# Second layer's mixer of a two-layer decoder: products of four blocks replaced by seven forms

## Chip, cores, metric

One NeuronCore of a Trainium2 chip runs the whole program. The metric is device time of one execution in microseconds (us), median of three runs. TensorE is PE in the rows, its weight loads PEld, VectorE DVE, ScalarE ACT, GpSimd POOL; SP issues the DMAs.

## The reference, cut to the part that changes

All is float32, 1024 tokens of width 1024. Layer 1 (the second) has a gated short convolution as its mixer:

```python
def short_conv_mixer(x, w_in, conv_w, w_out):          # layer 1
    proj = jnp.einsum('bsd,de->bse', x, w_in)          # 1024 x 1024 by 1024 x 3072
    gate_b, gate_c, h = jnp.split(proj, 3, axis=-1)
    z = gate_c * h
    zp = jnp.pad(z, ((0, 0), (CONV_WIDTH - 1, 0), (0, 0)))
    conv = sum(conv_w[k] * zp[:, k:k + s] for k in range(CONV_WIDTH))   # 3 taps
    return jnp.einsum('bse,ed->bsd', gate_b * conv, w_out)
...
for i in range(DEPTH):
    mix = ... if i % 2 == 0 else short_conv_mixer(...)
    x = layer_norm(DEEPNORM_ALPHA * x + mix, ln1_g[i], ln1_b[i])
    hid = jnp.square(jax.nn.relu(jnp.einsum('bsd,df->bsf', x, ffn_w1[i])))
    x = layer_norm(DEEPNORM_ALPHA * x + jnp.einsum('bsf,fd->bsd', hid, ffn_w2[i]), ln2_g[i], ln2_b[i])
    x = x + sigmoid(x @ ple_gate_w[i]) * (p[i] @ ple_w[i])
```

## The kernel before

**Products.** A float32 operand is split into a high part (ACT casts it to fp32r) and a low part (DVE or POOL subtracts the high part), and each 128x128 by 128x512 product is three matmuls: high by high, high by low, low by high (L1851 to L1853). Eight PSUM banks of 128x512 form two rings, `bank_a` and `bank_b`, of four.

**The two feed-forward layers** already use seven products in place of eight (a Strassen-Winograd scheme over 2x2 blocks). Their first product goes in *trips*: a trip makes 256 columns for all 1024 tokens by the seven products A11, S1, A22 (of the trip before), S2, A12, S4, S3, each 12 matmuls. The weight operand of each is one of the four quarters of the block (A..) or a sum of them (S..): S1 and S3 are summed on DVE, S2 and S4 on POOL; ACT makes the high part `op_hi`, POOL the low part `op_lo`. Five operand slots hold them, prepared four products ahead (`OP_LEAD`). The token operands are xt, its quarters, and four sums of them, `t_raw`/`t_hi`/`t_lo` 1 to 4. Three products accumulate on top of a bank that DVE must have read before, so PE waits: S4 for the read after S1, S3 for the read after S2, A22 for the second read of S3's bank. The results go to DRAM in seven forms (four quarters and three sums). Their second product is made of seven forms m1 to m7 whose operands are loaded back in *items* (`h_raw`, `w_raw`, split to `hop` and `wop`), five items in flight; m6, m5, m3 accumulate in the banks of the form before them, m4 in those of m7, so DVE must have added ("flushed") the form before to `resid` first.

**The mixer of layer 1** is done plainly before the change. For each of four blocks of 256 columns: gate_c (stage `c`, ACT copies it to `cv`), h (stage `h`, DVE multiplies and makes three taps of convolution), gate_b (stage `bgate`, DVE multiplies, splits into `hid_hi`, `hid_lo`), then the block's share of the output product goes to `bank_b` and DVE adds it to `resid` (stage `out`). Weight slabs are split by ACT (`w_hi`) and POOL (`w_lo`, L1007).

Each engine runs one list of stages in program order. An instruction that waits holds back all behind it on its engine. SP runs loads and spills in such a list as well.

```python
dve.tensor_tensor(z[:, k, o:o + HALF], bank_a[(st.ga + k) % RING][:, :], cv[:, k, s], ALU.mult)   # L1789
clink(dve.tensor_scalar(cv[:, k, s], z[:, k, o:o + HALF], tap[2], None, ALU.mult))                # L1792
clink(dve.scalar_tensor_tensor(out=cv[:, k, s], in0=z[:, k, o - 1:o - 1 + HALF], ...))            # L1793
clink(dve.scalar_tensor_tensor(out=cv[:, k, s], in0=z[:, k, o - 2:o - 2 + HALF], ...))            # L1795
```

## Time and profile before

| | |
|---|---|
| median of 3 runs | 2101.3 us (2101.21 to 2101.44) |
| span of the profiled execution | 2099.5 us, 25079 instructions |
| PE busy | 2088.8 us, 99%, 9605 instructions |
| DVE, ACT, POOL busy | 59%, 38%, 35% |
| mixer of layer 1 in the span | about 999 to 1354 us |
| mean granted TensorE clock | 1.000 |

For the profiled execution the profile gives its span alone; the median of the runs is 1.8 us above it. A matmul's busy time (389 ns) overlaps the next one's: what counts is the distance of their starts. The first column of a timeline row is its start in us, the second how long it took.

### The profile page before, as it was taken

How to read it: one execution, taken by the hardware profiler on the slowest of the kernel's cores; microseconds unless marked ns; L12 is line 12 of the kernel's file. 1: busy time of each engine (PE TensorE's matmuls, PEld its weight loads, DVE VectorE, ACT ScalarE, POOL GpSimd, SP SyncE). 2: the span in 40 equal slices, each digit the busy share in tenths (PEclk: the TensorE clock that was granted, in tenths of full speed). 3: DMA queues.
4: the chain of work that ended last, by engine and by line, in shares of the span. 5: the costliest groups of instructions: out<-in, count | busy, mean ns of one | idle time of the engine just before them, and what ended most of it. 6: DMA issues, size and time to landing. Idle time of an engine off the chain costs nothing.

```text
span 2099.5 us, 25079 instructions
## 1 busy us (share of the span) xinstructions
PE 2088.8 (99%) x9605; PEld 1735.1 (83%) x9605; DVE 1237.6 (59%) x1619; ACT 788.2 (38%) x1165; POOL 732.5 (35%) x493
## 2 busy tenths in 40 slices
PE   9999999999999999999999999999999999999999
PEld 9888788888888888888888888888888888888887
DVE  4744775565666657664543352675556566666563
ACT  3112454544543334531211101455444544334530
POOL 5113167778502000221422322268777512000220
PEclk9999999999999999999999999999999999999999
DMA  5111124344599555311121111124434599554221
GB/s 187 41 61 52 30 81 155 140 147 162 179 360 390 192 199 172 111 41 30 41 81 41 58 44 45 36 81 155 156 136 160 184 376 377 193 189 170 96 86 40
DMA packets 180819, 287.17 MB, mean 137 GB/s; under 512 B 12800, under 2 KB 71260, under 8 KB 180700
## 3 DMA queue, kind: packets, MB, share of 16 engines
q1 hardware_dynamic: 180000, 285.26, 39.6%
q8 instruction: 76, 1.25, 0.3%
q10 hardware_dynamic: 700, 0.31, 0.1%
q14 instruction: 43, 0.35, 0.1%
...
## 4 chain that ended last, share of the span: by engine, by line
PE 94%; POOL 2%; DVE 2%; issue 1%; ACT 1%; ACTq 0%; POOLq 0%; DVEq 0%
PE bank_a L1851 17%; PE bank_a L1853 17%; PE bank_a L1852 17%; PE bank_b L1851 14%; PE bank_b L1853 14%; PE bank_b L1852 14%; POOL op_lo L1021 1%; PE bank_a L1890 1%; PE bank_b L1890 1%; POOL op_sum L1094 1%; DVE xt_lo L1393 1%; DVE xt_hi L1388 0%; ACT op_hi L1249 0%; PE bank_a L2069 0%; PE bank_a L2078 0%
## 5 line engine op out<-in xcount | busy, mean ns | idle before, releaser
L1007 POOL TENSOR_TENSOR w_lo<-raw,w_hi 128x512 fp32r<-128x512 f32 x148 | 207.8, 1436 | 861.3 <-ACT w_hi L1115 861.2
L1851 PE MATMUL bank_a<-xt_hi,w_hi 128*128 128x512 f32 x640 | 251.4, 393 | 0.1
L1853 PE MATMUL bank_a<-xt_hi,w_lo 128*128 128x512 f32 x640 | 249.2, 389 | 0.0
L1852 PE MATMUL bank_a<-xt_lo,w_hi 128*128 128x512 f32 x640 | 249.1, 389 | 0.0
L1219 ACT CAST hop_hi<-h_raw 128x1024 fp32r<-128x1024 f32 x112 | 117.8, 1051 | 243.6 <-PE bank_a L1853 145.1
L1592 DVE TENSOR_TENSOR hop_lo<-h_raw,hop_hi 128x1024 fp32r<-128x1024 f32 x112 | 137.5, 1227 | 118.1 <-ACT hop_hi L1219 117.9
L1853 PE MATMUL bank_a<-wop_hi,hop_lo 128*128 128x512 f32 x512 | 199.2, 389 | 0.0
L1851 PE MATMUL bank_a<-wop_hi,hop_hi 128*128 128x512 f32 x512 | 199.2, 389 | 0.0
L1852 PE MATMUL bank_a<-wop_lo,hop_hi 128*128 128x512 f32 x512 | 199.2, 389 | 0.0
L1115 ACT CAST w_hi<-raw 128x512 fp32r<-128x512 f32 x148 | 82.4, 621 | 284.7 <-PE bank_a L1853 154.7
L1021 POOL TENSOR_TENSOR op_lo<-op_sum,op_hi 128x512 fp32r<-128x512 f32 x112 | 165.7, 1497 | 11.1 <-ACT op_hi L1249 6.7
L1249 ACT CAST op_hi<-op_sum 128x512 fp32r<-128x512 f32 x112 | 69.7, 622 | 227.1 <-POOL op_sum L1094 65.8
L1851 PE MATMUL bank_b<-wop_hi,hop_hi 128*128 128x512 f32 x384 | 150.0, 391 | 0.0
L1853 PE MATMUL bank_b<-wop_hi,hop_lo 128*128 128x512 f32 x384 | 149.5, 389 | 0.0
L1852 PE MATMUL bank_b<-wop_lo,hop_hi 128*128 128x512 f32 x384 | 149.4, 389 | 0.0
L1021 POOL TENSOR_TENSOR op_lo<-w_raw,op_hi 128x512 fp32r<-128x512 f32 x84 | 118.3, 1408 | 88.0 <-ACT op_hi L1249 87.0
L1851 PEld LDWEIGHTS bank_a<-xt_hi,w_hi 128*128 128x128 f32 x640 | 120.2, 188 | 26.1 <-DVE xt_lo L1393 0.9
L1853 PEld LDWEIGHTS bank_a<-xt_hi,w_lo 128*128 128x128 f32 x640 | 120.1, 188 | 25.2
L1852 PEld LDWEIGHTS bank_a<-xt_lo,w_hi 128*128 128x128 f32 x640 | 120.2, 188 | 24.7 <-issue 0.5
L1853 PE MATMUL bank_a<-xt_hi,op_lo 128*128 128x512 f32 x336 | 130.7, 389 | 0.0
L1851 PE MATMUL bank_a<-xt_hi,op_hi 128*128 128x512 f32 x336 | 130.7, 389 | 0.0
L1852 PE MATMUL bank_a<-xt_lo,op_hi 128*128 128x512 f32 x336 | 130.7, 389 | 0.0
...
## 6 DMA issues: line engine op xcount, KB each, us to landing
w_raw<-in_ffn_w_dram SPq DMA_DIRECT2D x144, 512.0 KB, 6.3
h_raw<-h_spill SPq DMA_DIRECT2D x112, 512.0 KB, 5.4
h_spill<-h_tile SPq DMA_DIRECT2D x170, 256.0 KB, 2.3
w_raw<-in_ffn_w_dram SPq DMA_DIRECT2D x112, 256.0 KB, 3.4
raw<-in_od_w_in_dram SPq DMA_DIRECT2D x48, 256.0 KB, 2.8
raw<-in_ple_gate_w_dram SPq DMA_DIRECT2D x32, 256.0 KB, 3.6
h_spill<-h_tile2t SPq DMA_DIRECT2D x28, 256.0 KB, 2.0
raw<-in_ev_w_in_dram SPq DMA_DIRECT2D x24, 256.0 KB, 3.2
```

Source lines behind the costliest of these rows:

```text
L1007: pool.tensor_tensor(lo, raw[:, n % NRAW, :], hi.bitcast(F32), ALU.subtract).then_inc(lo_split, 1)
L1021: pool.tensor_tensor(by_four(op_lo[s]), by_four(src) if src is not None else w1_quarter(b, op), by_four(op_hi[s]).bitcast(F32), ALU.subtra ...
L1094: pool.tensor_tensor(by_four(op_sum[s]), w1_quarter(b, "A12"), by_four(s2), ALU.subtract)\
L1115: act.copy(piece_place(slab, q)[0], raw[:, n % NRAW, :]).then_inc(hi_split, 1)
L1219: act.copy(hop_hi[k][:, :, :], h_raw[a.hop_chunk(i)][:, :, :]).then_inc(ahead_hi, 1)
L1249: act.copy(by_four(op_hi[s]), src).then_inc(op_high, 1)
L1393: dve.tensor_tensor(lo, staged(st, k), hi.bitcast(F32), ALU.subtract)\
L1592: dve.tensor_tensor(hop_lo[k][:, :, :], h_raw[a.hop_chunk(i)][:, :, :], hop_hi[k][:, :, :].bitcast(F32), ALU.subtract).then_inc(ahead_dve, 1)
L1851: pe.matmul(dst, s_hi, m_hi, start=first, stop=False, skip_group_check=on_top)
L1852: pe.matmul(dst, s_hi, m_lo, start=False, stop=False, skip_group_check=on_top)
L1853: return pe.matmul(dst, s_lo, m_hi, start=False, stop=last, skip_group_check=on_top)
L1890: ins = pe.transpose(dst[:, t * P:(t + 1) * P], src[:, st.half * HT + t, j * P:(j + 1) * P], ident[:, :])
```

## The change

The mixer of layer 1 takes the form of the feed-forward. The first 256 columns of gate_c and of h stay plain. The ten other blocks of the input product become trips, in the order b0, c1, h1, b1, c2, h2, b2, c3, h3, b3 (c: gate_c, h: h, b: gate_b, with the block's number). ACT and DVE evict each trip's quarters: c into `cv`, h into `z` (multiplied by `cv`, then 12 convolution instructions in the trip), b is multiplied by `cv`, and seven forms of it go to DRAM (`g_spill`). The output product is 14 items, two for each form. Trip b3 has S3 and S4 exchanged. The scaling of `resid` by alpha moves to POOL in trips 2 to 9, one tile in each.

```diff
+OD_TRIPS = (("b", 0),) + tuple((kind, blk) for blk in range(1, OD_BLOCKS) for kind in ("c", "h", "b"))
+OD_ITEMS = ([("m1", 0), ("m2", 0), ("m1", 1), ("m2", 1)]
+            + [(form, j) for form in ("m6", "m5", "m3", "m7", "m4") for j in range(OD_PAIRS)])
+OD_SLOTS = (0, 1, 2, 3, 4, 0, 1, 2, 3, 4, 0, 2, 1, 3)
...
+            per_trip = PER_TRIP if layer != OD or b < end - 1 else PER_TRIP[:5] + ("S3", "S4")
...
+    def short_conv():
+        turn = turns("gate", 1, list(range(KT)), ring="B", nested=True)
+        add("c", slab=("od", D), half=0, paced=True, split_next=True, inner=[turn])
+        add("tsum", layer=OD).unit = turn.unit
+        add("c", half=1, paced=True, last=True)
+        add("thi", layer=OD, half=1)
+        for i in (-4, -3, -2):
+            trip_step(OD, i)
+        add("thi", layer=OD, half=3)
+        add("h", slab=("od", 2 * D), half=1, load_next=False, split_next=False)
+        add("t4", layer=OD)
+        add("thi", layer=OD, half=2)
+        trip_step(OD, -1)
+        add("h", half=0, last=True)
+        for i, (b, op) in enumerate(tr.seq):
+            trip_step(OD, i)
+            if i == 1:
+                add("thi", layer=OD, half=4)
+            if op == "S2" and PLAIN < b <= PLAIN + TT:
+                add("alpha", tiles=[b - PLAIN - 1])
+            if b == last and op in ("S3", "S4"):
+                prepare(OD, ("S3", "S4").index(op))
+        nxt, form_heads = 2, {}
+        for i, (form, j) in enumerate(OD_ITEMS):
+            while nxt < len(OD_ITEMS) and (a.user_before(nxt) is None or a.user_before(nxt) < i):
+                prepare(OD, nxt)
+                nxt += 1
+            st = add("prod", item=i, layer=OD, head=form_heads.get(form))
...
-    for blk in range(OD_BLOCKS):
-        if blk == 0:
-            feature_halves("c", ("od", D), "gate")
-        else:
-            add("c", slab=("od", D + blk * BLK), half=0, blk=blk)
-            add("c", half=1, blk=blk, last=True)
-        add("h", slab=("od", 2 * D + blk * BLK), half=0, blk=blk)
-        add("h", half=1, blk=blk, last=True)
-        add("bgate", slab=("od", blk * BLK), half=0, blk=blk)
-        add("bgate", half=1, blk=blk, last=True)
-        block_out(("od_out", blk * BLK), ln=2 if blk == OD_BLOCKS - 1 else None)
+    short_conv()
...
+            def od_evictions(st):
+                if op == "S4":
+                    dve.wait_ge(trip_done, tr.done[b, op])
+                    od_wait(b, "u1")
+                    dve.tensor_tensor(q12, q12, bank, ALU.add).then_inc(od_step, 1)
+                    if kind == "h":
+                        od_wait(b, "c12")
+                        dve.tensor_tensor(q12, q12, cv_12[:, :], ALU.mult).then_inc(od_step, 1)
+                        od_wait(b, "m12")
+                        od_conv(b, blk, 0, 0)
+                        od_conv(b, blk, 0, 1)
```

Two places in DVE's program. First the h stage of the fourth block before and the same block's h trip after. Of before, `scratch` is both z and cv; two of four tiles are shown:

```order
L1789 TENSOR_TENSOR scratch<-bank_a,scratch 128x512
L1792 TENSOR_SCALAR scratch<-scratch,cols 128x512
L1793 SCALAR_TENSOR_TENSOR scratch<-scratch,cols 128x512
L1795 SCALAR_TENSOR_TENSOR scratch<-scratch,cols 128x512
L1789 TENSOR_TENSOR scratch<-bank_a,scratch 128x512
L1792 TENSOR_SCALAR scratch<-scratch,cols 128x512
L1793 SCALAR_TENSOR_TENSOR scratch<-scratch,cols 128x512
L1795 SCALAR_TENSOR_TENSOR scratch<-scratch,cols 128x512
```

After the change, from S4's eviction (`z<-z,bank_a`) to S3's (`z<-z,bank_b`) in an h trip:

```order
L1770 TENSOR_TENSOR z<-z,bank_a 128x512
L1773 TENSOR_TENSOR z<-z,cv_181 128x512
L1717 TENSOR_SCALAR cv_180<-z,cols 128x512
L1719 SCALAR_TENSOR_TENSOR cv_180<-z,cols,cv_180 128x512
L1722 SCALAR_TENSOR_TENSOR cv_180<-z,cols,cv_180 128x512
L1717 TENSOR_SCALAR cv_181<-z,cols 128x512
L1719 SCALAR_TENSOR_TENSOR cv_181<-z,cols,cv_181 128x512
L1722 SCALAR_TENSOR_TENSOR cv_181<-z,cols,cv_181 128x512
L1787 TENSOR_TENSOR z<-z,bank_b 128x512
L1791 TENSOR_TENSOR z<-z,cv_182 128x512
```

The read of S3's bank (`bank_b`) now stands behind one product with `cv` and six convolution instructions.

Second, the output product. Before, DVE comes from a gate_b stage straight to the 16 additions of a block:

```order
L1803 TENSOR_TENSOR tmp<-bank_a,scratch 128x512
L1388 CAST hid_hi<-tmp 128x512
L1393 TENSOR_TENSOR hid_lo<-tmp,hid_hi 128x512
L1636 TENSOR_TENSOR resid<-resid,bank_b 128x512 x16
L1789 TENSOR_TENSOR scratch<-bank_a,scratch 128x512
```

After, the rows ahead of the first flush, that of m1 (`t_od` is the weight sum of m6, `w_raw` with `t_od` that of m5, `hop_lo`, `wop_lo` the low parts of items 4, 5 and 6):

```order
L1978 TENSOR_TENSOR t_od_179<-w_raw_158,w_raw_164 128x1024
L1988 TENSOR_TENSOR hop_lo_138<-h_raw_153,hop_hi_133 128x1024
L1991 TENSOR_TENSOR wop_lo_148<-t_od_178,wop_hi_143 128x1024
L1980 TENSOR_TENSOR w_raw_159<-w_raw_159,t_od_178 128x1024
L1988 TENSOR_TENSOR hop_lo_134<-h_raw_154,hop_hi_129 128x1024
L1991 TENSOR_TENSOR wop_lo_144<-t_od_179,wop_hi_139 128x1024
L1980 TENSOR_TENSOR w_raw_160<-w_raw_160,t_od_179 128x1024
L1988 TENSOR_TENSOR hop_lo_135<-h_raw_155,hop_hi_130 128x1024
L1991 TENSOR_TENSOR wop_lo_145<-w_raw_159,wop_hi_140 128x1024
L2010 TENSOR_TENSOR resid<-resid,bank_a 128x512 x4
```

The flush now stands behind the preparation of items 2 to 6; the item that accumulates on its banks is item 4.

## Rows read from the trace of the kernel before

**Rows 1.** The page: span, and busy time of each engine.

```profile
span 2099.5 us, 25079 instructions
...
PE 2088.8 (99%) x9605; PEld 1735.1 (83%) x9605; DVE 1237.6 (59%) x1619; ACT 788.2 (38%) x1165; POOL 732.5 (35%) x493
```

**Rows 2.** Windows: mixer of layer 1, then trips of layer 0: busy per engine, clock.

```profile
1030.00:1340.00 310.00, 310.00 (x1370) 256.76 (x1369) 130.24 (x177) 42.43 (x76) 81.47 (x59) 1.00 0.18 54
360.00:555.00 195.00, 194.34 (x854) 159.23 (x853) 114.88 (x125) 96.56 (x165) 153.21 (x105) 1.00 0.45 156
```

**Rows 3.** PE's timeline in the mixer: first and last of 118 matmuls.

```profile
1014.66 0.39 PE L1851 MATMUL bank_a<-xt_hi,w_hi 128*128 128x512 f32 x1
...
1041.19 0.39 PE L1851 MATMUL bank_a<-xt_hi,w_hi 128*128 128x512 f32 x1
```

**Rows 4.** DVE's timeline: two tiles of the h stage, 1040 to 1053 us.

```profile
1042.17 0.49 DVE L1792 TENSOR_SCALAR scratch<-scratch,cols 128x512 f32<-128x512 f32 x1
1042.70 0.75 DVE L1793 SCALAR_TENSOR_TENSOR scratch<-scratch,cols 128x512 f32<-128x512 f32 x1
1043.49 0.75 DVE L1795 SCALAR_TENSOR_TENSOR scratch<-scratch,cols 128x512 f32<-128x512 f32 x1
...
1047.61 1.50 DVE L1792 TENSOR_SCALAR scratch<-scratch,cols 128x512 f32<-128x512 f32 x1
1049.14 1.66 DVE L1793 SCALAR_TENSOR_TENSOR scratch<-scratch,cols 128x512 f32<-128x512 f32 x1
1050.84 1.67 DVE L1795 SCALAR_TENSOR_TENSOR scratch<-scratch,cols 128x512 f32<-128x512 f32 x1
```

**Rows 5.** POOL's timeline over the same time: all of its work from 1028 to 1062.

```profile
1027.01 5.03 POOL L1007 TENSOR_TENSOR w_lo<-raw,w_hi 128x512 fp32r<-128x512 f32 x4
1047.53 6.13 POOL L1007 TENSOR_TENSOR w_lo<-raw,w_hi 128x512 fp32r<-128x512 f32 x4 [15.49 <-ACT w_hi L1115]
```

**Rows 6.** The chain that ended last, in one trip of layer 1's feed-forward.

```profile
1460.95 0.24 PE bank_a L1853
...
1461.25 0.60 ACT op_hi L1249
...
1461.92 1.35 POOL op_lo L1021
1463.27 1.71 POOL op_sum L1094
...
1465.04 1.64 POOL op_lo L1021
...
1466.82 0.47 PE bank_b L1851
```

**Rows 7.** DVE's timeline ahead of the trips of layer 1's feed-forward.

```profile
1392.62 5.49 DVE L1483 TENSOR_TENSOR t_raw<-xt_hi,t_raw 128x1024 f32<-128x1024 f32 x2 [8.57 <-PE bank_a L1853]
1398.15 5.55 DVE L1492 TENSOR_TENSOR t_lo<-t_raw,t_hi 128x1024 fp32r<-128x1024 f32 x2
1403.62 4.54 DVE L1498 TENSOR_TENSOR t_raw<-t_raw,xt_lo 128x1024 f32<-128x1024 f32 x2
...
1411.56 2.60 DVE L1492 TENSOR_TENSOR xt_lo<-t_raw,xt_hi 128x1024 fp32r<-128x1024 f32 x2 [1.10 <-ACT xt_hi L1129]
```

**Rows 8.** ACT's timeline there: the copies ahead of that last DVE row.

```profile
1410.47 2.00 ACT L1129 CAST xt_hi<-t_raw 128x1024 fp32r<-128x1024 f32 x2
```

**Rows 9.** DVE's timeline where layer 1's items are prepared.

```profile
1716.56 1.22 DVE L1595 TENSOR_TENSOR wop_lo<-w_raw,wop_hi 128x1024 fp32r<-128x1024 f32 x1
1717.70 1.22 DVE L1592 TENSOR_TENSOR hop_lo<-h_raw,hop_hi 128x1024 fp32r<-128x1024 f32 x1
```

**Rows 10.** DMA issues: KB each and median us to landing.

```profile
h_raw<-h_spill SPq DMA_DIRECT2D x112, 512.0 KB, 5.4
h_spill<-h_tile SPq DMA_DIRECT2D x170, 256.0 KB, 2.3
```

**Rows 11.** One load of six within five us, and the cast that waited for it.

```profile
1686.69 1.00 SPq L833 DMA_DIRECT2D h_raw<-h_spill  x1
...
1694.66 1.05 ACT L1219 CAST hop_hi<-h_raw 128x1024 fp32r<-128x1024 f32 x1 [0.35 <-DMA h_raw<-h_spill]
```

**Rows 12.** Windows at the end of the span, where PE has stopped: clock.

```profile
2097.00:2099.00 2.00, 0.00 (x0) 0.00 (x0) 0.05 (x1) 0.00 (x0) 0.00 (x0) 0.79 0.35 131
```

More of the change, by code:

```diff
@@ L213, in spilled, with pair, slot, hop_chunk @@
         return 16 * (self.layer * (FFN_BLOCKS - PLAIN) + blk - PLAIN + 1)
+class OdAhead(Ahead):
+    def pair(self, i):
+        return self.items[i][1]
+    def slot(self, i):
+        return OD_SLOTS[i]
+    def hop_chunk(self, i):
+        return OD_HOP_AT[i]
+    def w_chunk(self, load):
+        return OD_W_AT[load]
 class Trips:
@@ L242, in __init__ @@
             if op in ("S2", "S4"):
-                self.sum_pool[b, op] = layer * 2 * blocks + len(self.sum_pool) + 1
+                self.sum_pool[b, op] = base["sums"] + len(self.sum_pool) + 1
+            if op == "A11":
+                self.move[b] = base["moves"] + len(self.move) + 1
+            if layer == OD:
+                kind = OD_TRIPS[b - PLAIN][0]
+                for name in (OD_STEPS[kind] if b < end - 1 else OD_LAST).get(op, ()):
+                    self.step[b, name] = len(self.step) + 1
+                if op == "A12" and kind == "c":
+                    self.copied[b] = len(self.copied) + 1
+                continue
@@ new lines, in first_read, with make_trips, make_ahead @@
+    def first_read(self, b, op):
+        name = {"S4": "s15", "S3": "u1", "A22": "c22"}[op]
+        return ("odstep", self.step[b, name]) if self.layer == OD else ("hid", self.hid[b, name])
+def make_trips():
+    trips, before = {}, None
+    for layer, end in ((0, FFN_BLOCKS), (OD, PLAIN + len(OD_TRIPS)), (1, FFN_BLOCKS)):
+        trips[layer] = before = Trips(layer, before, end)
+    return trips
+def make_ahead():
+    first = FfnAhead(0, None, ITEMS, PAIRS, True)
+    mixer = OdAhead(OD, first, OD_ITEMS, OD_PAIRS, False)
+    return {0: first, OD: mixer, 1: FfnAhead(1, mixer, ITEMS, PAIRS, True)}
@@ L260, in make_plan @@
     held = {"A": [None] * RING, "B": [None] * RING}
-    trips = [Trips(layer) for layer in range(2)]
-    ahead = [Ahead(layer) for layer in range(2)]
+    trips, ahead = make_trips(), make_ahead()
     need = dict(xu=[0, 0], hu=[0, 0])
@@ L285, in add @@
         if kind == "prod" and args["head"] is None:
-            adds["ga" if FORMS[ITEMS[args["item"]][0]][0] == "A" else "gb"] = adds["flu"] = HT
+            adds["ga" if FORMS[ahead[args["layer"]].items[args["item"]][0]][0] == "A" else "gb"] = adds["flu"] = HT
         if args.get("ring") == "B":
@@ L452, in prepare @@
     def prepare(layer, n):
-        if n + 1 < len(ITEMS):
+        if n + 1 < len(ahead[layer].items):
             add("wsum", item=n + 1, layer=layer)
@@ L531, in trunk @@
     plan, trips, slab_end, slabs, total, ends = make_plan()
-    ahead = [Ahead(layer) for layer in range(2)]
-    heads = [{ITEMS[st.item][0]: st for st in plan if st.kind == "prod" and st.layer == layer and st.head is None}
-             for layer in range(2)]
+    ahead = make_ahead()
+    heads = {layer: {a.items[st.item][0]: st for st in plan
+                     if st.kind == "prod" and st.layer == layer and st.head is None} for layer, a in ahead.items()}
     n_slabs = total["slab"]
@@ L875, in stage @@
             def stage(st):
-                if st.kind == "slab":
+                if st.kind == "slab" and st.layer == OD:
+                    sp.wait_ge(ahead_dve, ahead[OD].sum[5])
+                elif st.kind == "slab":
                     sp.wait_ge(ahead_dve, ahead[st.layer].dve[LAST_FORM - 1])
@@ L1042, in stage @@
                     split_low(st.cur + 2, st.piece + 6, 4, at=1)
-                if st.kind == "wsum" and ITEMS[st.item][0] == "m6":
+                if st.kind == "wsum" and ahead[st.layer].items[st.item][0] == "m6":
                     a, i = ahead[st.layer], st.item
@@ L1596, in stage @@
                                       ALU.subtract).then_inc(ahead_dve, 1)
-                if st.kind == "prod" and ITEMS[st.item][1] == PAIRS - 1:
-                    form, head = ITEMS[st.item][0], st.head
+                if st.kind == "prod" and ahead[st.layer].items[st.item][1] == ahead[st.layer].pairs - 1:
+                    form, head = ahead[st.layer].items[st.item][0], st.head
                     if form == "m1":
```

583 lines of the change are left out of this document (425 added, 158 removed).

## The prediction

> **What bounds the kernel now.** I read the page first: PE is busy 2088.8 of 2099.5 us, and no other engine over 59% [rows 1]. The windows say the same of this mixer: 310 of 310 us busy, clock 1.00, with DVE at 42% and POOL at 26% [rows 2]. Then PE's timeline, for what a matmul costs. Its row says 389 ns, but the starts are closer: 118 matmuls in a row start between 1014.66 and 1041.19 us, 26.53 / 117 = 0.2267 us apart [rows 3]. That distance is the price of a matmul here, since PE issues one after another with no gap. In the whole mixer I found no pause of PE over 0.2 us. So a matmul removed from the mixer shortens the span in full, unless PE then waits, and every wait of PE is new time.
>
> **What is removed.** A plain block of the input product is 96 matmuls, a trip 7 x 12 = 84; ten blocks save 120. The output product goes from 384 to 14 x 24 = 336 and saves 48. The order confirms 168 fewer. 168 x 0.2267 = **38.1 us**. The plain mixer's casts and slab splits go too, but they lie beside PE and give nothing.
>
> **What is added** lies on DVE, POOL, ACT and SP. A product takes 12 x 0.2267 = 2.72 us and a trip 19.05 us, an item 5.44 us. I go through the four places where PE can come to wait.
>
> *DVE beside POOL.* The convolution shows its price twice: 0.49, 0.75 and 0.75 us with POOL idle, 1.50, 1.66 and 1.67 us at 1047 to 1052 [rows 4], when POOL works without a break [rows 5]. In the mixer before, that is rare. In trips POOL is busy 153.2 of 195 us, 79% [rows 2], so this is what the h trips run in. With starts 0.04 apart, a tile's three instructions are 2.1 us alone and 4.9 us beside POOL; two tiles at a share of 79% go at a speed of 0.21 + 0.79 x 2.1 / 4.9 = 0.55, so 4.2 / 0.55 = 7.6 us.
>
> The Trainium skill (SBUF — State Buffer, "Who interferes with whom") says that a VectorE instruction with two SBUF inputs and a GpSimd instruction that reads SBUF exclude each other for the whole instruction, the second one waiting until the first ends. The rows agree that both lose, but four of POOL's went from 5.03 to 6.13 us, and one of DVE's from 0.75 to 1.67. By the rule each of DVE's would wait out one of POOL's and take 1.26 + 0.75 = 2.0 us, two tiles some 9 us instead of 7.6, which over three h blocks is an estimated 4 us more.
>
> *1. The first trip: 8 us.* Ahead of the feed-forward's trips DVE needs 1392.62 to 1408.1 = 15.5 us for six large instructions, from the end of the third plain half block on [rows 7]. The new mixer has the same six at the same place (end of the first half of h), plus one z product ahead and two behind (0.6 each, a read of PSUM), then 12 convolution instructions, 8.4 us at the price alone, since POOL runs out of work then. Only behind them stand the sum for S3 and the eviction of S1: 15.5 + 1.8 + 8.4 + 1.2 = 26.9 us. PE has 10.9 us of the plain half block, then A11, S1, S2, A12, and wants S4 at 21.8. Wait 5.1. Behind it ACT makes S3's high part and two large copies of 2.0 us [rows 8], DVE the two `xt_lo` that follow (2.6) [rows 7] and the eviction of S2: S3 waits 2 to 3 more, and the next S1 some 0.5. Bounds: 5, if DVE's six go at their price alone (about 7 us); 11, if the convolution runs beside POOL.
>
> *2. The h trips: 7 us.* After S4 ends DVE does its eviction 0.6, the product 1.2, two tiles 7.6, then reads S3's bank 0.6: 10.0 us. A22 needs that read, and PE has three products, 8.16 us, until then: 1.9 us of wait, and some 0.4 on the operand of the next S1, whose sum is queued on DVE as well. The second half (behind A22: 0.6, 1.2, 7.6, 0.6 against 8.16 us until S3) has the slack that the first wait made. I take 2.3 for each of three blocks. Bounds: nothing at the price alone (0.6 + 0.7 + 4.2 + 0.6 = 6.1 < 8.16), and with POOL busy all the time 0.6 + 1.6 + 9.8 + 0.6 = 12.6, 4.4 us twice in a block, 26 us. In c and b trips DVE has 6 to 17 us of work in 19, so delays don't add up.
>
> *3. The last trip: 2.5 us.* In the feed-forward the path to S2's operand takes 1460.95+0.24 to 1466.82 = 5.6 us for two products of PE, 5.44: it is just at its limit [rows 6]. It goes through POOL's sum and two low parts. With S3 ahead of S4 the sum for S4 has its slot one product later, and S3's own low part, from DVE's sum, comes ahead on POOL: 1.2 + 0.6 + 1.35 + 1.71 + 1.64 and gaps of 0.3 are 6.8 after A11, with DVE late from h3: 1.4 to 3.5 us of wait.
>
> *4. The output product: 12 us.* Item 4 (m6) accumulates on m1's banks, and could start 4 x 5.44 = 21.8 us after the last A22. DVE must flush m1 first, in the order given, after preparing items 2 to 6. Item 3 needs the form that the last A22 makes: DVE reaches it about 5.6 us after A22 ends (three sums and item 1's preparation are ahead), the spill takes 2.3, its load 5.4 by the median [rows 10], but 1694.66 - 1686.69 = 8 when six are under way [rows 11], and here it is followed by six or more; with the cast that is 17.5 us. Then DVE works through item 3, the weight sums of 5, 6 and 7 and items 4, 5, 6: 11 instructions at 1.14 apart [rows 9], 12.5 us, so the first flush ends at 30.7: item 4 is 9 us late, of which 3.4 already at item 3. Weights of items 5 and 6, last in the same burst, may cost 1 or 2 more. Then DVE is behind, and m5, which needs m6's flush, waits about 2. Sum 12. Bounds: 4, if loads land at the median and nothing is ahead on DVE; 18, if the burst adds another 6. Afterwards DVE has some 9.5 us of work in 10.9 us of PE for each form and keeps up. The layer norm behind it follows the last additions by the same instructions as before, and costs nothing new.
>
> *5. The clock: 2 us.* Before, PE never paused; only when it had ended did the granted clock fall, to a mean of 0.79 in the window 2097 to 2099 [rows 12]. A pause of 6 to 9 us ahead of item 4 may let it fall too, to 1.2 GHz. From no fall (0) to a stretch at half speed as long as the pause (4.5): I take 2. The page TensorE: Matmul & The Clock Gate (The Trainium skill, "What's actually happening") gives 1.2 and 2.4 GHz as the two levels and idleness as what leads to the lower; no row here shows how it comes back.
>
> Sum: -38.1 + 8 + 7 + 2.5 + 12 + 2 = -6.6. The profiled span 2099.5 would become 2092.9, and the median, 1.8 above, **2094.7, say 2095 us**.
>
> **Rivals.** *The waits are mostly hidden* (0.15). POOL pauses whenever PE does, so DVE's work runs near the price alone, and loads land in time: 5 + 0 + 1.4 + 6 + 0 = 12.4, 26 us faster, about 2078; with half of that, 2085. Against it stands that in the trips POOL is busy 79% and that the order behind A22 is fixed.
>
> *The convolution beside POOL takes over* (0.20). Place: the h trips. If DVE is served at 4.9 us a tile throughout, the waits there are up to 26 in place of 7, the sum is +12 and the time 2114. It decides from where an h block costs over (38.1 + 4.2 - 24.5) / 3 = 5.9 us. For it: every DVE row beside a busy POOL is at the high price. Against it: POOL has only five slots of lead and must stop when PE stops.
>
> *Each pause costs the clock* (0.10, within the case above and the next). Seven pauses of 2 to 8 us; if PE then runs at half speed for as long as each, the 29.5 us of waits bring 15 more in place of 2, and the time is 2108.
>
> *Gain and waits cancel* (0.20): waits of 34 to 42 us, 2097 to 2105, by the upper half of the bounds of places 1 and 4.
>
> **How the numbers follow.** Within 0.2% (4.2 us) I could not tell a change. The forecast, 2085 to 2097, has 0.45, the hidden case 0.15: faster 0.6. Cancelling 0.2. Slower 0.2, from convolution and clock. The range leaves out about 0.1 on either side: 2081 to 2108; the likeliest case alone is 2085 to 2097.
>
> **What would show it.** PE 168 instructions fewer; PE idle of some 30 us in place of 2, with its releasers DVE evictions (S4, S3 of b0; A22 of h1 to h3), POOL's `op_lo` (S2 of b3), and ahead of items 3, 4 and m5 DVE's `wop_lo` and flush. The convolution's rows between 1.0 and 1.67 us in trips. The granted clock below 1.00 in a window behind item 4. Wrong it would be by convolution rows at 0.5 to 0.8 us, by an item 4 that starts with no wait, or by waits of PE for loads or spills in the trips, of which I see none.

## The result and the profile after

The changed kernel takes **2114.6 us** (median of 4 runs, 2113.2 to 2116.8), the kernel before 2101.3 on the same chip: a ratio of 1.0065, 95% interval 1.0051 to 1.0079. It is slower by 13.3 us, where 2095 was forecast. The page, beside [rows 1]:

```profile
span 2111.6 us, 25132 instructions
...
PE 2067.5 (98%) x9437; PEld 1712.4 (81%) x9437; DVE 1328.9 (63%) x1689; ACT 835.3 (40%) x1215; POOL 810.8 (38%) x533
```

PE has 9437 instructions, 168 fewer, and the gain of 38.1 us is real: its busy time fell by 21.3 us although much of what is left ran slower. It was paid back inside the mixer. Before, PE had no pause there. Now its timeline has eleven. Each row is the first matmul behind one; the bracket is the wait and what ended it (two of the eleven, 3.14 and 1.02 us, repeat those at 1124 and 1143 and are left out):

```profile
1031.89 0.80 PE L2232 MATMUL bank_a<-xt_hi,w_hi 128*128 128x512 f32 x1 [6.42 <-POOL w_lo L1246]
1068.06 0.50 PE L2232 MATMUL bank_a<-xt_hi,op_hi 128*128 128x512 f32 x1 [1.84 <-DVE b L1752]
1079.99 0.47 PE L2232 MATMUL bank_a<-t_hi,op_hi 128*128 128x512 f32 x1 [1.83 <-POOL op_lo L1260]
1124.20 0.79 PE L2232 MATMUL bank_b<-xt_hi,op_hi 128*128 128x512 f32 x1 [3.13 <-DVE z L1787]
1143.28 0.47 PE L2232 MATMUL bank_a<-t_hi,op_hi 128*128 128x512 f32 x1 [1.06 <-POOL op_lo L1260]
...
1248.15 0.50 PE L2232 MATMUL bank_b<-xt_hi,op_hi 128*128 128x512 f32 x1 [0.32 <-DVE z L1787]
1254.55 0.77 PE L2232 MATMUL bank_b<-t_hi,op_hi 128*128 128x512 f32 x1 [3.38 <-POOL op_lo L1260]
1290.61 0.56 PE L2232 MATMUL bank_b<-wop_hi,hop_hi 128*128 128x512 f32 x1 [3.20 <-DVE wop_lo L1991]
1305.97 0.77 PE L2232 MATMUL bank_a<-wop_hi,hop_hi 128*128 128x512 f32 x1 [8.03 <-DVE resid L2010]
```

The waits are 33.4 us. By the distances of starts, with 0.2267 taken off each, they are 35.1. The rest is behind them. PE's timeline after the wait of 3.13 us:

```profile
1124.80 0.63 PE L2233 MATMUL bank_b<-xt_lo,op_hi 128*128 128x512 f32 x1
1125.22 0.63 PE L2234 MATMUL bank_b<-xt_hi,op_lo 128*128 128x512 f32 x1
...
1127.46 0.40 PE L2234 MATMUL bank_b<-xt_hi,op_lo 128*128 128x512 f32 x1
1127.70 0.39 PE L2232 MATMUL bank_b<-xt_hi,op_hi 128*128 128x512 f32 x1
```

Matmuls start 0.43 us apart, not 0.23, from 1124.2 to 1127.2: half speed, 1.4 us lost. The same in the windows (columns: from and to, length, busy of PE, PEld, DVE, ACT, POOL with counts, granted clock, DMA share, GB/s):

```profile
1032.00:1040.00 8.00, 8.00 (x30) 6.52 (x31) 1.40 (x3) 1.25 (x2) 5.97 (x4) 0.82 0.43 133
1040.00:1055.00 15.00, 15.00 (x68) 12.43 (x67) 10.47 (x7) 1.14 (x2) 9.30 (x5) 1.00 0.00 0
...
1254.00:1262.00 8.00, 7.46 (x21) 5.92 (x22) 6.58 (x7) 1.84 (x2) 3.51 (x3) 0.61 0.10 23
...
1306.00:1312.00 6.00, 6.00 (x16) 4.73 (x17) 6.00 (x12) 0.00 (x0) 0.00 (x0) 0.55 1.04 393
1312.00:1320.00 8.00, 8.00 (x37) 6.62 (x36) 8.00 (x11) 2.31 (x3) 0.00 (x0) 1.00 0.93 325
```

From 1306 to 1312 PE is busy all the time and does 16 matmuls in 6 us, behind it 37 in 8. Seven pauses (the six of over 3 us and that of 1.84 us at 1068) have such a *slow stretch*: they lose 1.5, 1.7, 1.4, 1.6, 2.7, 1.7 and 2.6 us, 13.3 together. With some single slow starts, the loss against the kernel before is some 14 us in all (matmuls that start over 0.2267 us apart without a pause, summed over the span: some 24 us against 10). So -38.1 + 35.1 + 14 = +11, of 12.1 us by which the span of the profiled execution grew; 1 us of it isn't placed.

| place | us predicted | us in the trace |
|---|---|---|
| `h`'s slab, ahead of the trips | none | 6.4 |
| first trip | 8 | 3.7 |
| h trips | 7 | 8.7 |
| last trip | 2.5 | 3.4 |
| output product | 12 | 11.2 |
| clock | 2 | 13.3 to 14 |

**The pause nobody looked for.** PE waits 6.4 us for the low part of `h`'s slab. POOL's timeline there, four instructions of 128x512, and DVE's at the same time, eight sums of 128x1024:

```profile
1015.88 15.96 POOL L1246 TENSOR_TENSOR w_lo<-raw,w_hi 128x512 fp32r<-128x512 f32 x4 [64.52 <-ACT w_hi L1354]
```

```profile
1017.88 2.35 DVE L1850 TENSOR_TENSOR t_raw<-t_raw,xt_hi 128x1024 f32<-128x1024 f32 x2
...
1024.69 2.35 DVE L1864 TENSOR_TENSOR t_raw<-tmp,t_raw 128x1024 f32<-128x1024 f32 x2
```

POOL's four took 5.0 to 6.1 us before [rows 5] and take 16.0 here. The mean of 4.0 hides how: windows of POOL alone (busy time with count, granted clock, DMA) over this row:

```profile
1015.90:1028.10 12.20, 12.20 (x1) 1.00 0.00 0
1028.20:1031.80 3.60, 3.60 (x3) 0.50 0.00 0
```

The first of the four takes 12.3 us, from 1015.9 to 1028.2, and ends 1.1 us after the last of DVE's sums (1027.0); the other three take 1.26 each. So one instruction was held for as long as DVE had such work without a gap. DVE loses nothing: 1.14 us for each sum. In [rows 4] it was DVE that lost most.

**In an h trip** DVE's timeline from S4's eviction to the read of S3's bank, the order shown ahead of the prediction:

```profile
1112.95 0.69 DVE L1770 TENSOR_TENSOR z<-z,bank_a 128x512 f32<-128x512 f32 x1 [2.03 <-PE bank_a L2234]
...
1114.87 1.40 DVE L1717 TENSOR_SCALAR cv<-z,cols 128x512 f32<-128x512 f32 x1
1116.31 0.75 DVE L1719 SCALAR_TENSOR_TENSOR cv<-z,cols,cv 128x512 f32<-128x512 f32 x1
1117.09 1.66 DVE L1722 SCALAR_TENSOR_TENSOR cv<-z,cols,cv 128x512 f32<-128x512 f32 x1
...
1123.47 0.67 DVE L1787 TENSOR_TENSOR z<-z,bank_b 128x512 f32<-128x512 f32 x1
```

Six convolution instructions take 8.6 us here (7.6 were forecast), the next six 4.7.

**In the output product**, ahead of item 4, DVE:

```profile
1289.32 1.23 DVE L1991 TENSOR_TENSOR wop_lo<-w_raw,wop_hi 128x1024 fp32r<-128x1024 f32 x1
1294.92 1.23 DVE L1978 TENSOR_TENSOR t_od<-w_raw,w_raw 128x1024 f32<-128x1024 f32 x1 [4.37 <-POOL w_raw L1287]
...
1304.01 1.21 DVE L1991 TENSOR_TENSOR wop_lo<-w_raw,wop_hi 128x1024 fp32r<-128x1024 f32 x1
1305.15 2.47 DVE L2010 TENSOR_TENSOR resid<-resid,bank_a 128x512 f32<-128x512 f32 x4
```

DVE stands still for 4.4 us for a weight that landed late (POOL's sum of it starts only at 1292.4), does nine instructions for items 4 to 7, and only then flushes m1, which PE had finished at 1287.

### The profile page after: what moved, and what is told of

Its sections match the earlier page's. It is cut to its first block and busy times, and to the rows that moved or that the text cites. A ratio compares the mean times of both kernels' runs of the same rounds, so it can differ in the third digit from the quotient of the medians.

```text
span 2111.6 us, 25132 instructions
## 1 busy us (share of the span) xinstructions
PE 2067.5 (98%) x9437; PEld 1712.4 (81%) x9437; DVE 1328.9 (63%) x1689; ACT 835.3 (40%) x1215; POOL 810.8 (38%) x533
## 5 line engine op out<-in xcount | busy, mean ns | idle before, releaser
L1246 POOL TENSOR_TENSOR w_lo<-raw,w_hi 128x512 fp32r<-128x512 f32 x92 | 140.7, 1561 | 736.3 <-ACT w_hi L1354 736.3
L1260 POOL TENSOR_TENSOR op_lo<-op_sum,op_hi 128x512 fp32r<-128x512 f32 x152 | 222.5, 1480 | 42.6 <-ACT op_hi L1525 36.6
L2232 PE MATMUL bank_a<-xt_hi,op_hi 128*128 128x512 f32 x456 | 178.3, 391 | 1.8 <-DVE b L1752 1.8
L2233 PE MATMUL bank_a<-xt_lo,op_hi 128*128 128x512 f32 x456 | 178.1, 391 | 0.0
L2232 PE MATMUL bank_a<-xt_hi,w_hi 128*128 128x512 f32 x320 | 127.6, 399 | 6.4 <-POOL w_lo L1246 6.4
L2232 PEld LDWEIGHTS bank_a<-wop_hi,hop_hi 128*128 128x128 f32 x576 | 108.8, 189 | 30.8 <-DVE wop_lo L1991 8.4
L1991 DVE TENSOR_TENSOR wop_lo<-w_raw,wop_hi 128x1024 fp32r<-128x1024 f32 x108 | 132.6, 1228 | 0.6
L2233 PEld LDWEIGHTS bank_a<-wop_lo,hop_hi 128*128 128x128 f32 x576 | 108.8, 189 | 22.7
L2234 PEld LDWEIGHTS bank_a<-wop_hi,hop_lo 128*128 128x128 f32 x576 | 108.7, 189 | 22.8
L2232 PE MATMUL bank_b<-t_hi,op_hi 128*128 128x512 f32 x304 | 120.4, 396 | 5.0 <-POOL op_lo L1260 4.9
```

Source lines behind the costliest of these rows:

```text
L1246: pool.tensor_tensor(lo, raw[:, n % NRAW, :], hi.bitcast(F32), ALU.subtract).then_inc(lo_split, 1)
L1260: pool.tensor_tensor(by_four(op_lo[s]), by_four(src) if src is not None else w1_quarter(b, op), by_four(op_hi[s]).bitcast(F32), ALU.subtra ...
L1991: dve.tensor_tensor(wop_lo[k][:, :, :], w2_source(a, i), wop_hi[k][:, :, :].bitcast(F32), ALU.subtract).then_inc(ahead_dve, 1)
L2232: pe.matmul(dst, s_hi, m_hi, start=first, stop=False, skip_group_check=on_top)
L2233: pe.matmul(dst, s_hi, m_lo, start=False, stop=False, skip_group_check=on_top)
L2234: return pe.matmul(dst, s_lo, m_hi, start=False, stop=last, skip_group_check=on_top)
```

## Experiments

The theory: each wait is a place in the order of DVE's or POOL's queue, and each pause of some length has a slow stretch of its own. The rivals: DVE's (or the loads') sum of work is the limit, so that a wait removed comes back elsewhere; and the clock's loss is something else than the pause.

### Four edits of order, one at a time

**Flush m1 ahead of items 4 to 6.**

```diff
-            while nxt < len(OD_ITEMS) and (a.user_before(nxt) is None or a.user_before(nxt) < i):
+            while nxt < len(OD_ITEMS) and (a.user_before(nxt) is None or a.user_before(nxt) < i) \
+                    and not (nxt >= 4 and i < 3):
```

> DVE flushes m1 right behind the preparation of item 3; items 4, 5 and 6 are prepared behind it. Theory (item 4 waits for the flush's place in DVE's order): item 3 ends as before; DVE is done with item 3 at 1290.6 us, flushes m1 until 1293.0, must then still wait for the weight sum of item 5 (POOL, at 1294.9), and has item 4 ready at 1298.4, so PE's wait ahead of item 4 falls from 8.0 to about 2.3 us, and with it the slow stretch behind it (2.6 us over full speed) to 1 or less: 2107 us. Rival A (the clock costs nothing of its own, only waits count): 2109 us. Rival B (the late loads hold item 4, not the order): the wait stays at 8 and the time at 2114.6.

Measured: 2113.7 us (2110.2 to 2114.2), ratio to before 1.0054 (1.0037 to 1.0071). PE's waits at items 4 and 6:

```profile
1299.61 0.50 PE L2233 MATMUL bank_a<-wop_hi,hop_hi 128*128 128x512 f32 x1 [0.56 <-DVE wop_lo L1992]
...
1317.50 0.77 PE L2233 MATMUL bank_a<-wop_hi,hop_hi 128*128 128x512 f32 x1 [6.71 <-DVE resid L2011]
```

The place was right, 8.0 became 0.6. But the flush of m6 stands behind items 7 and 8 and m2's flush in the same queue, and PE, now earlier, meets it.

**In the h trips, read S3's bank ahead of the convolution**, and the last quarter of it behind S2's read of the b trip.

```diff
...
                         dve.tensor_tensor(q12, q12, cv_12[:, :], ALU.mult).then_inc(od_step, 1)
-                        od_wait(b, "m12")
-                        od_conv(b, blk, 0, 0)
-                        od_conv(b, blk, 0, 1)
...
                         dve.tensor_tensor(q22, q22, cv_22[:, :], ALU.mult).then_inc(od_step, 1)
+                        od_wait(b, "m12")
+                        od_conv(b, blk, 0, 0)
+                        od_conv(b, blk, 0, 1)
...
```

> In the h trips the convolution of the first half stands behind the read of S3's bank, and the last quarter of the convolution behind the first read of the next trip's S2. Same instructions, other order. Theory (the order of the reads costs the 3.1 + 3.1 + 0.3 us ahead of A22 and the 1.1 + 1.0 ahead of the next S1, and each 3.1 us wait a slow stretch of 1.4 to 1.6 us behind it): all of it goes, 8.6 + 3.0 us: 2103 us. Rival (DVE as a whole is the limit in an h trip, so the wait only moves to the next read or operand sum): 2112 to 2115 us, with PE released by DVE at other lines.

Measured: 2116.8 us (2115.7 to 2118.5), 1.0075 (1.0060 to 1.0090). The waits of 3.13 us ahead of A22 are gone, and waits of 0.8 and 3.4 us stand in their place, the second for POOL's low part of the next S1: its sum, on DVE, was behind nine convolution instructions. As the rival said of the place, though the convolution in quarters, further down, shows that it was order all the same. Behind the wait of 3.40 us at 1144.9 no slow stretch follows, behind the next, 3.37 us at 1206.9, one of 1.7 us does.

**Undo the exchange in the last trip** (S4 ahead of S3 again).

```diff
-            per_trip = PER_TRIP if layer != OD or b < end - 1 else PER_TRIP[:5] + ("S3", "S4")
+            per_trip = PER_TRIP
...
```

> The last trip has S4 ahead of S3 again, like all others; preparation of items 0 and 1, spills and loads keep their places in time. Theory (the exchange puts S2's operand on a path of 6.8 us against 5.44): the 3.4 us wait ahead of S2 of b3 and the slow stretch of 2.7 us behind it go: 2108.5 us. Rival (that wait is DVE's and POOL's delay out of h3, not the exchange): wait of 2 to 3.4 us stays, 2113 to 2115 us. Another: the spills and items behind come later by as much as was won, and item 3 waits 6 us in place of 3: no change.

Measured: 2114.3 us (2114.1 to 2115.9), 1.0064 (1.0049 to 1.0079), no change. The 3.38 us ahead of S2 of b3 are gone, but these stand in PE's timeline, at A22 of h3 (0.32 before) and A22 of b3 (none before):

```profile
1251.04 0.80 PE L2229 MATMUL bank_b<-xt_hi,op_hi 128*128 128x512 f32 x1 [3.13 <-DVE z L1785]
1269.37 0.50 PE L2229 MATMUL bank_b<-xt_hi,op_hi 128*128 128x512 f32 x1 [1.73 <-DVE b L1785]
```

**DVE's eight sums behind POOL's split.**

```diff
                     if st.layer == OD:
                         dve.wait_ge(unit_lo, st.need_x[0])
+                        dve.wait_ge(lo_split, st.piece + 4)
```

> DVE starts the eight sums for t_raw only when POOL has split the h slab. Theory (POOL's four splits take 16 us because DVE's 128x1024 sums stand beside them; alone they take about 1.25 each): POOL is done at 1021, PE has no wait ahead of the first h matmul (6.4 us less) and no slow stretch behind it (1.5 less), and DVE, idle from 1027 to 1037.8 before, loses nothing: 2106.7 us. Rival (that wait paid in advance for the first trip, whose waits of 2.1, 1.8 and 1.8 us now grow by as much, since DVE's work there sets the end): 2113 to 2116 us.

Measured: 2110.2 us (2108.2 to 2111.8), 1.0042 (1.0027 to 1.0057). POOL's row, and PE's waits in the first trip:

```profile
1014.99 6.95 POOL L1246 TENSOR_TENSOR w_lo<-raw,w_hi 128x512 fp32r<-128x512 f32 x4 [64.53 <-ACT w_hi L1354]
```

```profile
1054.83 0.47 PE L2233 MATMUL bank_b<-t_hi,op_hi 128*128 128x512 f32 x1 [3.06 <-POOL op_lo L1260]
1064.60 0.50 PE L2233 MATMUL bank_a<-xt_hi,op_hi 128*128 128x512 f32 x1 [2.42 <-DVE b L1752]
1076.58 0.47 PE L2233 MATMUL bank_a<-t_hi,op_hi 128*128 128x512 f32 x1 [1.70 <-POOL op_lo L1260]
```

The four splits take 7.0 in place of 16.0 us by this edit alone, and the pause of 6.4 us is gone: DVE's sums had starved POOL. (The first still takes 3.2 us: DVE's subtractions ahead of the sums go on until 1017.1, and it ends 1.1 us behind them.) The first trip's waits rose from 3.7 to 7.2 us, so about half was an advance payment. Between the two theories: 4.4 us won, of 7.9.

### Further along the same queues

**Convolution of block 0 behind S2's read of the first trip**, on top of the last one.

```diff
+            if i == 2:
+                add("conv0")
...
```

> The edit of the run with the sums behind the split, and besides it the twelve convolution instructions of block 0 stand behind the read of S2's bank of the first trip, not ahead of S3's operand sum and of the read of S1's bank. Theory (those twelve, 11 us from 1052 to 1063, are what S4 and the next S1 wait for, 2.4 and 1.7 us): both waits and the slow stretches behind them go, about 6 us against that run's 2110.2: 2104 us; a wait of 3 us ahead of the first S2 stays, since it is for POOL's low part. Rival (DVE's sum of work up to the second trip is the limit, whatever its order): the waits come back at S3, A22 or the next S1, and the time is 2109 to 2111 us.

Measured: 2111.9 us (2110.8 to 2116.3), 1.0057 (1.0042 to 1.0072). The theory fell, and the rival named the place rightly: the read of S1's bank makes nobody wait any more, but twelve instructions in one piece now stand ahead of the next S1's sum, and PE waits 5.2 us there in place of 1.7. That DVE's sum of work is the limit doesn't follow: with the same instructions in quarters ("More of the same order", below) the two waits of this part are 4.1 and 1.1 us.

**Spread the convolution of the h trips**, a quarter at a time, over the h and the b trip.

```diff
+def conv_tiles(b, op, kind, end):
+    if kind == "h":
+        return ("10", "11") if op == "A22" and b == end - 2 else ()
...
+    return {"S1": ("01",), "A12": ("10",) if b < end - 1 else (), "S4": ("11",) if b < end - 1 else ()}.get(op, ())
```

> The convolution of an h trip is spread: one quarter behind S3's eviction, one behind S1's of the b trip, one behind A12's and one behind S4's there (in h3 the last two stay where they are). Same instructions. In the run with the convolution later, the operand sum for the next S1 came at 1137.6 instead of 1128, behind nine convolution instructions, and PE waited 3.4 us for the low part made from it. Theory (order, not amount: in an h and a b trip together DVE has work for about 31 of 38 us): no operand sum or bank read stands behind more than three convolution instructions, so the waits of the h trips (3.1, 1.1, 3.1, 1.0, 0.3) go with their slow stretches (3.0): 2103 us, or 2106 if the wait ahead of S2 of b3 grows. Rival (DVE beside POOL is too slow for any order): 2113 to 2117 us.

Measured: 2106.5 us (2104.8 to 2108.7), 1.0026 (1.0016 to 1.0036). The waits of the first two h blocks, 8.4 us, are down to 1.67 twice, behind which no slow stretch follows. The window of h1 and b1, of the changed kernel, then of this one:

```profile
1106.00:1163.00 57.00, 52.81 (x226) 42.88 (x225) 40.58 (x42) 12.68 (x22) 37.92 (x27) 0.97 0.27 87
```

```profile
1106.00:1163.00 57.00, 55.33 (x244) 45.52 (x243) 39.91 (x43) 14.57 (x25) 41.70 (x30) 1.00 0.27 88
```

18 matmuls more in the same 57 us, with DVE busy for 40 of them in both: order, not amount.

**Both flushes**, m1's and m6's, ahead of what isn't needed yet (`and not (nxt >= 8 and i < 6)` besides).

> As in the run with the flush first, and besides it items 8 and later are prepared only behind the flush of m6. In that run the wait of 8.0 us ahead of item 4 fell to 0.6, but 6.7 us came up ahead of item 6, which accumulates on m6's banks, flushed only behind items 7 and 8 and m2. Theory (order in DVE's queue): the flush of m6 now comes at 1311, and item 6 waits about 1 us; sum of both waits 1.6 in place of 8.0, with 2 us of slow stretch less: 2106 us. Rival (DVE has 25 us of work without a break from 1296 on, so what is pushed back is late at the next place): a wait of 4 to 6 us ahead of item 7, 8 or 9, 2112 us.

Measured: 2113.7 us (2108.1 to 2113.9), 1.0053 (1.0036 to 1.0070). The waits at items 4 and 6 are 0 and 0.9 us, as expected, and one of 3.5 us comes up at m4, whose banks hold m7: DVE had the layer norm's statistics of the first tiles ahead of m7's flush and waited for ACT's squares. The output product waits 7.9 us in place of 11.2. That isn't to be seen in the time: in the same trace the slow stretches of the trips are longer (2.8 and 3.0 us behind the pauses of 3.13 us, where the changed kernel's trace has 1.4 and 1.6). The edit doesn't touch the trips; what makes them longer isn't shown.

**All four together.**

> The four edits of order together: sums behind the split, convolution of block 0 behind S2's read, convolution of the h trips spread, both flushes ahead of later items. Nothing is computed otherwise. If the waits are separate costs, the gains add: 4.4 + 6 + 9 to 12 + 8.5 = 28 to 31 us, 2084 to 2087 us, faster than the kernel before by 0.7%, and the gain from 168 matmuls fewer is there to see. Rival (DVE's backlog is handed from place to place, so that each wait removed shows up behind): 2095 to 2105 us.

Measured: 2100.9 us (2098.8 to 2102.5), 0.9999 (0.9990 to 1.0008). 14 us less than the change, half of the forecast. 26.7 us of waits are left by the starts' distance, among them those that the single edits had created.

### The clock, measured by itself

**Eight long pauses in the kernel before.** POOL makes 2 to 14 small instructions on unused memory when a stage ends, and PE waits for them:

```diff
+                if (st.kind, st.half, st.blk) in PAUSES:
+                    pool.wait_ge(a_full, st.ga)
+                    for n in range(PAUSES[st.kind, st.half, st.blk]):
+                        pool.wait_ge(paused, before_pause(st) + n)
+                        pool.tensor_scalar(sig[:, 0, :], sig[:, 0, :], 1.0, 1.0, ALU.mult, ALU.mult)\
+                            .then_inc(paused, 1)
...
+                if (st.kind, st.half, st.blk) in PAUSES:
+                    pe.wait_ge(paused, before_pause(st) + PAUSES[st.kind, st.half, st.blk])
```

> The kernel before, with eight pauses of PE put into its mixer, two per block (ahead of h and of gate_b), the rest as it was: PE waits until POOL has made 2, 3, 4, 5, 6, 8, 10 and 14 instructions of some 0.55 us on unused memory behind the end of the stage before, 52 in all, some 30 us of pause. Theory (a pause of about 3 us or more costs a stretch at half clock of 3 to 6.5 us, whatever its length, 1.5 to 2.9 us): six or seven of the eight have one, about 14 us in all: 2101 + 30 + 14 = 2145 us. Rival A (the prediction's: a stretch as long as the pause, or none for short ones, with the mean 2 us in 30): 2133 us. Rival B (half clock for as long as each pause, so the loss grows with it): 2101 + 30 + 15, with 0.5 us behind the shortest and 4 behind the longest.

Measured: 2207.8 us (2205.8 to 2209.2), 1.0506 (1.0491 to 1.0522). POOL splits a slab ahead of its small instructions, which the expectation forgot, so the pauses are 8.4 to 16.5 us, 88.4 in sum. The shortest and the longest in PE's timeline, and windows behind them:

```profile
1032.67 0.79 PE L1866 MATMUL bank_a<-xt_hi,w_hi 128*128 128x512 f32 x1 [8.35 <-POOL sig L1047]
...
1413.61 0.80 PE L1866 MATMUL bank_a<-xt_hi,w_hi 128*128 128x512 f32 x1 [16.50 <-POOL sig L1047]
```

```profile
1032.50:1038.50 6.00, 5.83 (x14) 4.57 (x15) 0.00 (x0) 0.00 (x0) 0.11 (x1) 0.50 0.13 39
1413.50:1417.50 4.00, 3.89 (x9) 3.12 (x10) 0.00 (x0) 0.00 (x0) 0.06 (x1) 0.50 0.00 0
1418.00:1425.00 7.00, 7.00 (x33) 5.76 (x32) 1.81 (x3) 0.00 (x0) 0.00 (x0) 1.00 0.01 2
```

Behind all eight PE runs at 0.50 of 2.4 GHz, 1.2 GHz, for 3.1 to 6.1 us, then at 1.00. In order of the pauses (8.4, 8.8, 8.9, 10.2, 10.3, 12.3, 13.1, 16.5) the losses are 3.0, 1.6, 2.8, 2.4, 2.6, 2.9, 1.5, 2.0 us, some 18.7 together. They don't grow with the pause: rival B falls, and so does A. The forecast times all fell short, since the pauses came to 88 us and not 30; 2101 + 88 + 19 = 2208 us is what was measured.

**Sixteen pauses, meant short.** The same edit, three instructions at each of sixteen places.

> The kernel before with the same sum of pause in sixteen short ones: three POOL instructions, about 1.9 us, ahead of each half of h and of gate_b in all four blocks. Theory (a pause of up to 2 us has no slow stretch behind it): 16 x 1.9 = 30 us and no loss of clock: 2131 us, granted clock 1.00. Rival (the loss goes with the time paused): as much as with the long ones, 2145 us.

Measured: 2219.3 us (2216.9 to 2220.9), 1.0561 (1.0545 to 1.0577). For the same reason only the eight at second halves are short, 2.2 and 2.7 us by turns, so the test of 1.9 us isn't made. Behind the eight of 8.2 to 9.1 us there is always a slow stretch, behind those of 2.7 us three times in four, of 2.2 us once in four. Windows behind pauses of 2.21, 2.21 and 2.73 us:

```profile
1049.00:1052.50 3.50, 3.37 (x8) 2.70 (x9) 1.36 (x2) 0.00 (x0) 0.07 (x1) 0.52 0.00 0
1168.90:1172.40 3.50, 3.50 (x15) 2.91 (x16) 1.23 (x2) 0.00 (x0) 0.00 (x0) 1.00 0.00 0
...
1319.00:1322.50 3.50, 3.32 (x8) 2.67 (x9) 0.00 (x0) 0.00 (x0) 0.13 (x1) 0.54 0.00 0
```

**The long pauses filled** with unused products (beside the kernel with empty pauses; `FILL` is 34 to 70 products):

```diff
+                    pe.wait_ge(b_free, st.bread)
+                    for _ in range(FILL[st.kind, st.half, st.blk]):
+                        pe.matmul(bank_b[RING - 1][:, :], xt_hi[0][:, 0, 0:P], xt_hi[0][:, 0, :], start=True, stop=True)
                     pe.wait_ge(paused, before_pause(st) + PAUSES[st.kind, st.half, st.blk])
```

> The kernel before with the eight long pauses (8.4 to 16.5 us, 90 us in all, 2207.8 us, eight slow stretches of 1.5 to 3.0 us behind them, 17 us together), and in each pause PE makes 34 to 70 unused products of 128x128 by 128x512 on a free PSUM bank before it waits, so that it stands still for about 0.5 us only. Nothing else changes, and the wait ends at the same instruction of POOL. Theory (the slow stretches come from PE's standing still): granted clock 1.00 behind the pauses, 17 us less, 2191 us. Rival (the stretches come with the stop and start of the stage, or from POOL's and DVE's work there): 2207 us, stretches as before.

Measured: 2192.7 us (2191.8 to 2194.0), 1.0437 (1.0423 to 1.0451); the span is 17.3 us less than with empty pauses, and the window behind the first pause reads:

```profile
1032.50:1038.50 6.00, 6.00 (x27) 4.96 (x27) 0.36 (x1) 0.00 (x0) 0.00 (x0) 1.00 0.10 37
```

27 matmuls where there were 14, and no slow stretch in the whole mixer. POOL, ACT and DVE do the same as before (763.9, 788.6 and 1234.3 us busy, against 764.3, 788.6 and 1235.2 with empty pauses), and each pause keeps an empty rest of 0.7 to 0.9 us. So PE's standing still is the cause.

### A version that is faster than both

**More of the same order**: block 0's convolution in quarters; POOL's low part of the third token sum a step later; in the b trips the last quarter behind the read of S3's bank; h3's two quarters behind S2's read in the last trip; the statistics behind m7's flush.

```diff
+            if i in (2, 3, 4, 6):
+                add("conv0", item=(2, 3, 4, 6).index(i))
...
             if OD_ITEMS[i] == ("m3", OD_PAIRS - 1):
                 squares_of(lo)
+            if OD_ITEMS[i] == ("m7", OD_PAIRS - 1):
                 add("stats", half=0, ln=2)
                 add("norm", half=0, ln=2)
...
```

> As the run with all four edits of order, and more of the kind: the convolution of block 0 in quarters behind the steps S2, A12, S4 and the next A11; POOL's low part of the third token sum behind the first trip's A11 step, so that the low part for S2 isn't behind it; in the b trips the last quarter behind the read of S3's bank; in the last trip the two quarters of h3 behind the read of S2's bank; and the statistics of the first four tiles behind the flush of m7. Waits left in that run: 3.3, 5.2, 1.7, 1.7, 2.3, 2.0, 3.4, 2.2, 3.5 us = 25 and 11 us of slow stretches. Theory (all of them are places in DVE's or POOL's order): what is left is item 3's and 4's load, 3.4 and 2.2, and up to 1.5 at three places, with one slow stretch: 2100.9 - 15 - 8 = 2078 us. Rival (DVE's backlog comes back at other places, as it did with the flush first): 2090 to 2098 us.

Measured: 2087.1 us (2086.3 to 2088.2), 0.9931 (0.9915 to 0.9948): 14 us less than all four, of 23 expected. Waits left 17.7 us by starts, among them one of 4.1 us at the next S1 and 5.7 at item 3.

**The same without the exchange in the last trip.**

> The same, with the last trip's S4 ahead of S3 again. With h3's convolution out of the way, the exchange is all that holds S2 of b3 (2.3 us in the run before). Theory: S2 of b3 waits 0 and A22 of b3, which follows S3 at once, 1.7 for the read of its bank, too short for a slow stretch: 2 to 3 us less than the run beside it, 2076 us. Rival (items 0 to 4 are released by the forms of b3, so it makes no difference): the same time within 1 us.

Measured: 2085.0 us (2083.9 to 2087.5), **0.9924 (0.9909 to 0.9939)**. The difference of 2.1 us to the run beside it fits the theory, but the ranges of the two overlap, and A22 of b3 waits 3.1 us, not 1.7: its row and those of items 3 and 4 in PE's timeline:

```profile
1247.10 0.79 PE L2258 MATMUL bank_b<-xt_hi,op_hi 128*128 128x512 f32 x1 [3.08 <-DVE b L1802]
...
1270.42 0.50 PE L2258 MATMUL bank_b<-wop_hi,hop_hi 128*128 128x512 f32 x1 [1.22 <-DVE wop_lo L2011]
...
1280.29 0.79 PE L2258 MATMUL bank_a<-wop_hi,hop_hi 128*128 128x512 f32 x1 [4.13 <-DVE wop_lo L2011]
```

**Two of its pauses filled**, with 14 and 10 unused products, beside the same kernel again.

> The last kernel of order (2085.0 us) with 14 unused products ahead of S1 of c1 and 10 ahead of A22 of b3, where PE waited 4.1 and 3.1 us and slow stretches of 2.3 and 2.9 us followed. Theory: the waits stay, and the stretches go: 5 us less, 2080 us. Rival (unused products only move the wait, since DVE or POOL is slower beside a busy PE): 2085 us.

> The last kernel of order once more, on the same chip as the filled one, for a comparison of a few us: 2085 us.

Measured: 2084.7 us (2084.0 to 2084.9) filled, 2085.1 (2083.8 to 2086.2) again; 0.9922 (0.9908 to 0.9935) and 0.9925 (0.9912 to 0.9937). Both slow stretches are gone from the trace, and the time is the same. Two waits took their place: 1.31 us for DVE at 1074, and at item 3 4.13 us, where the unfilled kernel waits 1.1 to 1.2. Behind the second stands a new slow stretch of 2.9 us. PE's row, and the window behind it:

```profile
1269.69 0.79 PE L2262 MATMUL bank_b<-wop_hi,hop_hi 128*128 128x512 f32 x1 [4.13 <-DVE wop_lo L2015]
```

```profile
1269.70:1275.70 6.00, 6.00 (x14) 4.71 (x15) 3.84 (x6) 1.78 (x3) 2.37 (x1) 0.51 1.05 391
```

PE comes to item 3 earlier (1265.2 against 1268.8), and the item is ready at about the same time (1269.7 and 1270.4). That it is the load that sets this is argued from what DVE waits for, not tried. At item 6 both kernels wait about a microsecond for the same flush by DVE and go on at 1290.1 and 1290.5. So here what the fill won was taken back by later waits, and one of these brought a slow stretch of its own.

## Why the prediction was wrong

**Right.** 168 matmuls fewer and 38.1 us for them. The places of the waits, but for the one at the slab, and their releasers; the waits forecast at S3 of b0 and at m5 did not come. Their sizes: h trips 8.7 us for 7, last trip 3.4 for 2.5, output product 11.2 for 12, with 3.2 at item 3 for the late load and 8.0 at item 4 for the flush in its given order. No spill or weight load ahead of the output product held PE, as forecast.

**Wrong: step 5, "The clock: 2 us".** It looked at one pause, that of item 4, and asked whether the clock falls there. The trace has seven slow stretches of 1.4 to 2.7 us, 13.3 us. The pause kernels show the price of each: 1.5 to 3.0 us where there is one, whatever the length from 2.2 to 16.5 us; and filled pauses show the cause. In the prediction this stood as a rival with a chance of 0.10, its 15 us right, its reason (a stretch as long as its pause) not. That its 15 us come near the 13.3 is luck. The mechanism was named and the term mis-sized, by more than the whole forecast gain of 6.6 us.

**Wrong: "I go through the four places where PE can come to wait".** There was a fifth, ahead of the trips: POOL's split of `h`'s slab beside DVE's eight sums, 6.4 us. The prediction priced DVE's work beside POOL from [rows 4] and looked nowhere at POOL's beside DVE's large sums. [rows 5], 5.03 against 6.13 us, seemed to say that POOL hardly loses. The rule that it quoted from the Trainium skill (SBUF — State Buffer, "Who interferes with whom"), exclusive access for a whole instruction, with the second one blocked, agrees with these rows better than the mean factor taken from [rows 4]: beside eight DVE sums without a gap POOL's four took 16.0 us, 12.3 of them for the first alone, which ended only behind the last of the sums; without them the four took 7.0. The estimate made from the rule let a blocked instruction wait out one of the other engine's; this one waited out all eight sums and what stood ahead of them.

**Step 1, first trip: 8 us, measured 3.7.** Here one error covered the other. With the pause at the slab taken away, the first trip waits 3.1 + 2.4 + 1.7 = 7.2 us. In the changed kernel the pause of 6.4 us had given DVE and POOL the time. Together the two places are 10.1 us.

**Step 3** had the last trip's size, but the exchange isn't its cause: without it the waits are 3.1 and 1.7 us elsewhere.

By terms, against the forecast of -6.6: slab +6.4, first trip -4.3, h trips +1.7, last trip +0.9, output product -0.8, clock +11.3 to +12, and 1.7 by which the distances of the starts exceed the waits in brackets: 17 to 18 us, which makes +10.3 to +11 of the 12.1 seen. The range, 2081 to 2108, was too narrow above for two of these: the clock was bounded by 4.5 us for one pause, and with its term alone put right the forecast would have been 2106; the slab's wait, less what it saved in the first trip, and the smaller terms take it out of the range.

Two of its sums don't come out as written: the hidden case, -38.1 + 12.4, gives 2076 and not 2078 us, and the way to item 3, 5.6 + 2.3 + 8 and a cast of 1.05, gives 17.0 and not 17.5. Neither bears on the outcome.

**Where the expected gain went.** Not to an engine that is too slow: with the same instructions in another order the kernel takes 2085.0 us, 16 less than before and 30 less than the change. It went into DVE's and POOL's order, and 13 to 14 us besides into the clock, behind the pauses that this order made.
